# A row of norm weights spread by two matmuls with ones, in place of a load into all partitions

## The chip, the cores and the metric

One core of one Trainium2 chip runs the whole kernel. The metric is the device time of one execution in microseconds (us), of which the median over runs is given. The profile is one execution's, taken by the hardware profiler.

## The reference

One layer of a hybrid decoder trunk. 16 learned meta tokens are put ahead of 1,024 tokens of 1,024 channels; every token is normalised, and all groups (difference attention, a short gated convolution, a Mamba-2 scan) read the result through one projection:

```python
def rmsnorm(x, w):
    xf = x.astype(jnp.float32)
    y = xf * lax.rsqrt(jnp.mean(xf * xf, axis=-1, keepdims=True) + NORM_EPS)
    return (y * w.astype(jnp.float32)).astype(x.dtype)
...
    h = jnp.concatenate([meta, x], axis=1)
    for layer in range(DEPTH):
        u = rmsnorm(h, norm_w[layer])
        proj = jnp.einsum('bld,de->ble', u, w_in[layer])
...
        y = jnp.concatenate([y_attn, y_conv, y_ssm], axis=-1)
        h = h + jnp.einsum('ble,ed->bld', y, w_out[layer])
    return rmsnorm(h, final_norm_w)[:, N_META:]
```

`norm_w` is one row of 1,024 float32 values (4 KB), and every token's row is multiplied by it. Everything is float32 at the interface.

## The kernel before, in words

The program has three parts: a token stage that is run once (the table `AHEAD`), a loop of four iterations over heads (`BODY` three times and `LAST`), and the output projection. Each engine walks the same table in order and takes from it the steps that are its own; an engine never changes that order, and semaphores do the rest.

The token stage turns the tokens into the transposed, normalised matrix that all projections read, as a high part `u_hi` and a low part `u_lo`. It works on nine token tiles, numbered 0 to 8: tile 0 is the 16 meta tokens, tiles 1 to 8 have 128 tokens each, one per partition. For tile `a` the steps are:

- `x_load` (SP, L756): the DMA of the tile into `x_buf[a]`, 512 KB (64 KB for tile 0). The buffers are parts of `acum_b`, `work`, `lm_buf` and `ys`, and have these names in the profile.
- `x_square` (ScalarE, L1000): squares, summed along the row.
- `x_mean` (VectorE, L1202): 1/1024 of the sum, plus epsilon.
- `x_power` (GpSimd, L895): to the power -1/2.
- `x_scale` (VectorE, L1208): the tile times this factor, times `norm_row`, the norm's weights, which must be there in every partition. Called the first scaling for tile 0, the second for tile 1.
- `x_turn` (TensorE, L1584): eight transposes into PSUM.
- `x_high` (ScalarE, L1007) and `x_low` (VectorE, L1212): `u_hi` and `u_lo`.

`ahead()` writes the table: first the loads, in the order in which SP issues them, then rounds `r`, in each of which `PIPE` puts the steps of neighbouring tiles side by side (`x_square` three tiles ahead, `x_mean` and `x_power` two, `x_scale` and `x_turn` one). `BETWEEN` adds the first weight tiles and the first projections (`project`, L1599, into the PSUM banks `pb[0]` and `pb[1]`).

```python
PIPE = (("x_high", 0), ("x_square", 3), ("x_scale", 1), ("x_mean", 2), ("x_low", 0), ("x_power", 2), ("x_turn", 1))
```

`norm_row` is a part of `conv_u`, filled by the step `norm_load` (SP, L758), a DMA that writes the 4 KB row into all 128 partitions. Only the first scaling waits for it (`norm_in`). The constants (identity, `ones` and others) are written by GpSimd at the start, each adding one to `consts`; TensorE waits for all eight before its first instruction.

Of the kernel before, what the change touches and what calls it, by code (L numbers as in the profile page):

```python
# [15 lines left out]
P = 128  # L16
D = 1024
# [18 lines left out]
HALF = D // 2  # L36
# [119 lines left out]


def ahead():
    out = [("x_load", 0, 1), ("x_load", 1, 1), ("norm_load", 0, 1), ("x_load", 2, 1), ("x_load", 3, 1), ("load", 0, 1),
           ("x_load", 4, 1), ("load", 1, 1), ("w_dt_load", 0, 1)]  # L160
    out += [("x_load", a, 1) for a in range(5, CH)] + [("params_load", 0, 1)]
    for r in range(-3, CH):
        for name, lead in PIPE:
            if 0 <= r + lead < CH:
                out.append((name, r + lead, 1))
        out += [(name, arg, 1) for name, arg, at in BETWEEN if at == r]
    return out + [(name, arg, 1) for name, arg in BEHIND]

# [180 lines left out]
BODY = schedule(False)  # L349
LAST = schedule(True)  # L350
AHEAD = ahead()
DVE_OWN = 76
class Chain:
# [30 lines left out]
def build(nc, x, meta_tokens, norm_w, w_in, w_out, attn_lambda, attn_norm_w, sconv_w, ssm_conv_w,  # L384
# [6 lines left out]
    with ExitStack() as ctx:  # L391
        def sb(name, shape, dt=F32):
            return ctx.enter_context(nc.sbuf_tensor(name, shape, dt))

        def sem(name):
            return ctx.enter_context(nc.semaphore(name))
# [51 lines left out]
        th_piece = sb("th_piece", [P, 2, T // 2])  # L448
# [40 lines left out]
        s_tmp = [ys[:, n, HALF * m:HALF * (m + 1)] for n in range(2) for m in range(2)]  # L489

        norm_row = gate[:, 0:D]

        x_buf = [acum_b[:, :, :, :].rearrange("p b r n -> p (b r n)"), prob[0], prob[1], xs_flat[:, 0:LP], xs_flat[:, LP:2 * LP],
                 raw[:, 3:3 + LP], lm_buf[:, 3:3 + LP], ys[:, 0, :], ys[:, 1, :]]
# [5 lines left out]
        ones = sb("ones", [P, P])  # L500
# [50 lines left out]
        pb = [ps[:, 0, :], ps[:, 1, :]]  # L551
# [12 lines left out]
        params_in = sem("params_in")  # L564
        x_in = [sem(f"x_in{b}") for b in range(CH)]
        norm_in = sem("norm_in")
        w_dt_in = sem("w_dt_in")
        consts = sem("consts")
        x_sq = sem("x_sq")
# [144 lines left out]
        def _(eng):  # L714
# [24 lines left out]
            def iteration(i, steps):  # L739
                for step, a, d in steps:  # L740
# [12 lines left out]
                    elif step == "x_load":  # L753
                        n = META if a == 0 else P
                        src = meta_tokens if a == 0 else x_rows[(a - 1) * P:a * P, :]
                        eng.dma_start(x_buf[a][0:n, 0:D], src).then_inc(x_in[a], 16)  # L756
                    elif step == "norm_load":
                        eng.dma_start(norm_row, norm_w[0, :].partition_broadcast(P)).then_inc(norm_in, 16)  # L758
                    elif step == "w_dt_load":
                        eng.dma_start(w_dt, w_in_t[:, :, C_DT:C_DT + SH]).then_inc(w_dt_in, 16)  # L760
                    elif step == "params_load":
# [55 lines left out]
                    elif step == "t_store":  # L817
                        j = it * T_PAIRS + a
                        eng.wait_ge(t_ok, 4 * j + 4)
                        for m, name in enumerate(SUMS):  # L820
                            row = (m * KS + j) * P
                            eng.dma_start(t_dram[row:row + P, :], t_buf[name]).then_inc(t_st, 16)

            iteration(-1, AHEAD)
            for i in range(0, HEADS - 1):
                iteration(i, BODY)
            iteration(HEADS - 1, LAST)


# [123 lines left out]
        def _(eng):  # L953
# [24 lines left out]
            def iteration(i, steps):  # L978
                for step, a, d in steps:
                    it = i + d  # L980
                    if step == "split":
# [8 lines left out]
                        if a in SHARED:  # L990
                            eng.copy(w_hi[:, b, 0:KD // 2, :], w_raw[:, b, 0:KD // 2, :]).then_inc(w_half_ok, 1)
                            eng.copy(w_hi[:, b, KD // 2:KD, :], w_raw[:, b, KD // 2:KD, :]).then_inc(w_hi_ok, 1)
                        else:
                            eng.copy(w_hi[:, b, :, :], w_raw[:, b, :, :]).then_inc(w_hi_ok, 1)  # L994
                    elif step == "x_square":
                        n = META if a == 0 else P
                        eng.wait_ge(x_in[a], 16)
# [68 lines left out]
                    elif step == "gate_taps":  # L1066
                        n = a - TXS0
# [9 lines left out]
                    elif step == "exp":  # L1077
                        s, m = a
# [23 lines left out]
                    elif step == "z":  # L1102
                        p = PZ + a - 1
                        eng.wait_ge(piece_done, it * PPI + p + 2)
                        eng.activation(th_piece[:, p % 2, 0:GW], pb[p % 2][:, 0:GW], ACT.Tanh, scale=0.5).then_inc(zth_ok, 1)
                    elif step == "norm":
                        n = it * QB + a
# [5 lines left out]
                    elif step == "ssm_out":  # L1113
                        n = it * QB + a
# [6 lines left out]
                    elif step == "out_slot":  # L1121
# [4 lines left out]
                        high_w(a)  # L1126

            iteration(-1, AHEAD)
            for i in range(0, HEADS - 1):
                iteration(i, BODY)  # L1130
            iteration(HEADS - 1, LAST)

            def square(t, second):
# [39 lines left out]
        def _(eng):  # L1173
# [18 lines left out]
            def iteration(i, steps):  # L1192
                for step, a, d in steps:
                    it = i + d
                    if step == "parameters":

                        eng.wait_ge(par_tr, 1)
                        own(eng, eng.tensor_copy(par[:, :], o_ps[:, 0:R_END]))
                    elif step == "x_mean":
                        n = META if a == 0 else P  # L1200
                        eng.wait_ge(x_sq, a + 1)
                        eng.tensor_scalar(ms[0:n, a:a + 1], ss[0:n, a:a + 1], 1.0 / D, EPS, ALU.mult, ALU.add).then_inc(x_ms, 1)  # L1202
                    elif step == "x_scale":
                        n = META if a == 0 else P
                        eng.wait_ge(x_rs, a + 1)
                        if a == 0:
                            eng.wait_ge(norm_in, 16)
                        eng.scalar_tensor_tensor(x_buf[a][0:n, 0:D], x_buf[a][0:n, 0:D], rs[0:n, a:a + 1], norm_row[0:n, :], ALU.mult, ALU.mult).then_inc(x_n, 1)  # L1208
                    elif step == "x_low":
                        ca, cb = token_cols(a)  # L1210
# [127 lines left out]
                    elif step == "taps":  # L1338
                        t, j = a
                        n = t - TXS0  # L1340
# [15 lines left out]
                    elif step == "gate_taps":  # L1356
                        n = a - TXS0
# [6 lines left out]
                    elif step == "scores":  # L1364
                        s, m = a
                        nk = P * (s + 1) + META
                        n = it * 2 * QB + 2 * s + m
# [68 lines left out]
                    elif step == "chunk":  # L1436

                        n = META if a == 0 else P
# [19 lines left out]
                    elif step == "z":  # L1458

                        p = PZ + a - 1  # L1460
# [6 lines left out]
                    elif step == "scan":  # L1467
# [7 lines left out]
                        if a > 0:  # L1475
# [7 lines left out]
                            p = PZ + a - 1  # L1483
# [5 lines left out]
                    elif step == "norm":  # L1489

                        eng.wait_ge(z_sq, it * QB + a)
                        eng.tensor_scalar(z_ms[:, a % 2:a % 2 + 1], z_ss[:, a % 2:a % 2 + 1], 0.25 / GW, EPS, ALU.mult, ALU.add).then_inc(z_ms_ok, 1)

            iteration(-1, AHEAD)
            for i in range(0, HEADS - 1):
                own.begin(i)
                iteration(i, BODY)
                own.end()
            own.begin(HEADS - 1)
            iteration(HEADS - 1, LAST)  # L1500
            own.end()

# [49 lines left out]
            for n in range(5, 7 * KS):  # L1552
                p, j = n // KS, n % KS
# [28 lines left out]
        def _(eng):  # L1582
# [62 lines left out]
            def iteration(i, steps):  # L1645
                for step, a, d in steps:
                    it = i + d
                    if step == "project":
                        p, h = a
# [19 lines left out]
                                      range(h * KD // 2, (h + 1) * KD // 2))  # L1669
                        if h == 1:  # L1670
                            ins.then_inc(piece_done, 1)
                    elif step == "x_turn":
                        n = META if a == 0 else P
                        eng.wait_ge(x_n, a + 1)
# [52 lines left out]
                    elif step == "scores":  # L1727
                        s, m = a
                        n = it * 2 * QB + 2 * s + m
# [42 lines left out]
                    elif step == "chunk":  # L1772
                        n = META if a == 0 else P
# [13 lines left out]
                    elif step == "z":  # L1787

                        p = PZ + a - 1
# [12 lines left out]
                    elif step == "scan":  # L1802
                        n = META if a == 0 else P
# [23 lines left out]
                    elif step == "ssm_out":  # L1827
# [3 lines left out]
                        turn(yt_ps[:, P:2 * P], y_n[:, a % 2, P:2 * P]).then_inc(y_tr, 1)  # L1831

            iteration(-1, AHEAD)
            for i in range(0, HEADS - 1):
                iteration(i, BODY)
            iteration(HEADS - 1, LAST)


# [30 lines left out]
```

## Time and profile before

| | us |
|---|---|
| median of 3 runs | 1050.74 (1050.49 to 1052.12) |
| profiled execution | 1049.79 |
| its span | 1048.1 |
| TensorE busy in the span | 1013.8 (97%) |
| VectorE busy | 665.6 (64%) |
| ScalarE busy | 401.8 (38%) |
| GpSimd busy | 253.8 (24%) |

The span runs from the first to the last recorded instruction; the profiled execution's own time is 1.69 us longer. Times within the profile count from the start of the span. PE is TensorE's matmul, PEld its weight load, DVE VectorE, ACT ScalarE, POOL GpSimd, and SPq the queue of SyncE that issues DMAs. L12 is line 12 of the kernel. A matmul's duration is modelled to its end and overlaps the next one's; the distance between two starts tells the rate.

### The profile page before, as it was taken

The page shows a single profiled execution, that of the slowest core. Times are in us where ns is not written, and L with a number is a line of the kernel's source. Part 1 is how long each engine was busy: PE and PEld are TensorE (multiplying, and loading weights), DVE is VectorE, ACT ScalarE, POOL GpSimd, SP SyncE. Part 2 cuts the span into 40 slices and gives each one's busy share as a digit, 9 for nine tenths or more (in the row PEclk, how much of TensorE's full clock was granted, in tenths as well). Part 3 has the DMA queues.
Part 4 walks back from the last instruction along what each step waited for, and adds up shares of the span by engine and source line. Part 5 has one row for each costly group of instructions (what it writes and reads, how often), then busy time and mean ns, then how long its engine had stood idle before and what let it go on. Part 6 is the DMA issues. An engine that isn't in the chain of part 4 may idle for free.

```text
span 1048.1 us, 16326 instructions
## 1 busy us (share of the span) xinstructions
PE 1013.8 (97%) x6177; PEld 924.9 (88%) x6177; DVE 665.6 (64%) x1327; ACT 401.8 (38%) x892; POOL 253.8 (24%) x222
## 2 busy tenths in 40 slices
PE   4999999999999999999999999999999999999996
PEld 3889989898999898989999989899999898888885
DVE  7555767557257674672576756724767646798866
ACT  6333442233444332334343222343442233544554
POOL 3012331333223312332224133222241330000002
PEclk9999999999999999999999999999999999999999
DMA  8012322221142222211422322114223203994313
GB/s 268 1 44 81 101 81 71 71 61 44 47 133 101 71 81 71 61 41 41 141 84 76 93 71 61 42 41 141 76 70 101 71 20 105 359 389 140 100 51 161
DMA packets 105945, 101.22 MB, mean 97 GB/s; under 512 B 6022, under 2 KB 79852, under 8 KB 105868
## 3 DMA queue, kind: packets, MB, share of 16 engines
q1 hardware_dynamic: 105868, 100.18, 30.0%
q8 instruction: 50, 0.82, 0.3%
q14 instruction: 27, 0.22, 0.1%
HBM read 79.11 MB, written 21.05 MB: 96 GB/s over the span
## 4 chain that ended last, share of the span: by engine, by line
PE 84%; DVE 7%; issue 3%; DMA 2%; ACT 2%; POOL 1%; SPq 0%; POOLq 0%; DVEq 0%; ACTq 0%
PE ps L1599 43%; PE ps L1608 13%; PE ps L1800 9%; PE ps L1584 5%; PE ps L1765 3%; DVE lm_buf L1433 2%; PE ps L1814 2%; DMA acum_b<-acum_scratch 2%; PE ps L1743 2%; PE ps L1744 2%; PE ps L1816 1%; PE ps L1820 1%; PE ps L1691 1%; PE ps L1766 1%; DMA conv_u<-in_norm_w 1%
## 5 line engine op out<-in xcount | busy, mean ns | idle before, releaser
L1599 PE MATMUL ps<-u_hi,w_hi 128*128 128x348 f32 (+3 forms) x1024 | 364.4, 356 | 6.7 <-ACT conv_b_s L1053 2.5
L1599 PE MATMUL ps<-u_lo,w_hi 128*128 128x348 f32 (+3 forms) x1024 | 348.3, 340 | 0.0
L1599 PE MATMUL ps<-u_hi,w_lo 128*128 128x348 f32 (+3 forms) x1024 | 347.7, 340 | 0.0
L1599 PEld LDWEIGHTS ps<-u_hi,w_hi 128*128 128x128 f32 x1024 | 194.0, 189 | 19.8 <-issue 5.5
L904 POOL TENSOR_TENSOR w_lo<-w_raw,w_hi 128x1024 fp32r<-128x1024 f32 (+1 forms) x56 | 123.1, 2197 | 346.2 <-ACT w_hi L994 274.4
L1599 PEld LDWEIGHTS ps<-u_hi,w_lo 128*128 128x128 f32 x1024 | 193.3, 189 | 10.9
L1599 PEld LDWEIGHTS ps<-u_lo,w_hi 128*128 128x128 f32 x1024 | 193.7, 189 | 10.3
L895 POOL TENSOR_TENSOR small<-small,m_half 128x1 f32<-128x1 f32 (+2 forms) x57 | 41.5, 729 | 338.9 <-DVE small L1545 144.8
L1372 DVE TENSOR_REDUCE small<-ps 128x1 f32<-128x144 f32 (+7 forms) x64 | 49.5, 774 | 95.8 <-PE ps L1747 95.3
L1800 PE MATMUL ps<-w_hi,u_hi 128*128 128x256 f32 x256 | 73.1, 286 | 0.0
L1800 PE MATMUL ps<-w_lo,u_hi 128*128 128x256 f32 x256 | 72.0, 281 | 0.0
L1800 PE MATMUL ps<-w_hi,u_lo 128*128 128x256 f32 x256 | 72.0, 281 | 0.0
L1086 ACT ACTIVATE work<-ps,small 128x144 f32<-128x144 f32 (+7 forms) x64 | 48.0, 751 | 53.7 <-DVE small L1372 53.7
L1584 PE MATMUL ps<-ident,work 128*128 128x128 f32 (+2 forms) x369 | 56.6, 288 | 6.1 <-DVE work L1208 6.1
L1608 PE MATMUL ps<-q_hl 128*128 128x512 f32 x264 | 62.1, 389 | 0.0
L1433 DVE TENSOR_SCALAR lm_buf<-acum_b,sg 128x128 f32<-128x128 f32 x128 | 44.5, 409 | 27.5 <-DMA acum_b<-acum_scratch 27.5
L1101 ACT ACTIVATE lm_buf<-lm_buf 128x512 f32<-128x512 f32 x32 | 20.2, 632 | 107.0 <-DVE lm_buf L1433 107.0
L1112 ACT ACTIVATE y_n<-y_n,small 128x256 f32<-128x256 f32 x32 | 16.3, 510 | 112.9 <-POOL small L895 112.9
L1608 PEld LDWEIGHTS ps<-q_hl 128*128 128x128 f32 x264 | 49.6, 188 | 10.3
L1584 PEld LDWEIGHTS ps<-ident,work 128*128 128x128 f32 (+2 forms) x369 | 44.4, 143 | 9.9 <-DVE work L1208 7.8
L1456 DVE TENSOR_TENSOR lm_buf<-lm_buf,cbm 128x512 f32<-128x512 f32 x32 | 22.6, 707 | 43.3 <-PE ps L1820 43.1
L994 ACT CAST w_hi<-w_raw 128x1024 fp32r<-128x1024 f32 x48 | 49.9, 1040 | 0.1
(302 smaller groups left out, 1768.7 us busy)
## 6 DMA issues: line engine op xcount, KB each, us to landing
w_raw<-in_w_in SPq DMA_DIRECT2D x56, 512.0 KB, 4.1
acum_b<-acum_scratch SPq DMA_DIRECT2D x32, 256.0 KB, 4.4
acum_b<-in_w_out SPq DMA_DIRECT2D x22, 256.0 KB, 4.3
work<-in_w_out SPq DMA_DIRECT2D x16, 256.0 KB, 4.0
t_scratch<-work SPq DMA_DIRECT2D x16, 256.0 KB, 2.3
t_scratch<-acum_b SPq DMA_DIRECT2D x16, 256.0 KB, 2.6
y_scratch<-ys SPq DMA_DIRECT2D x8, 512.0 KB, 4.0
work<-in_x SPq DMA_DIRECT2D x4, 1024.0 KB, 8.4
```

The lines of the kernel that those rows point to most:

```text
L895: return eng.tensor_tensor(to[0:rows_, n:n + w], of[0:rows_, n:n + w], m_half[0:rows_, 0:w], ALU.pow)
L904: eng.tensor_tensor(w_lo[:, a % 2, ks, :], w_raw[:, a % 2, ks, :], w_hi[:, a % 2, ks, :].bitcast(F32), ALU.subtract).then_inc(w_lo_ok, 1)
L994: eng.copy(w_hi[:, b, :, :], w_raw[:, b, :, :]).then_inc(w_hi_ok, 1)
L1086: eng.activation(prob[m][:, 0:nk], s_ps[:, 0:nk], ACT.Exp, bias=mx[:, m:m + 1], accum_out=psum_e[:, s % 2, m:m + 1]).then_inc(exp_ok, 1)
L1372: eng.tensor_reduce(mx[:, m:m + 1], s_ps[:, 0:nk], AX.X, ALU.max, negate=True).then_inc(max_ok, 1)
L1433: ins = eng.tensor_scalar(lmat[:, a % 2, r, :], acum_b[:, a % 2, r, :], sg[:, 1, a, r:r + 1], 0.0, ALU.subtract, ALU.min)
L1456: eng.tensor_tensor(lmat[:, b, :, :], lmat[:, b, :, :], cbm[:, b, :].unsqueeze(1).to_broadcast([P, R, P]), ALU.mult).then_inc(g_ok, 1)
L1584: return eng.transpose(dst, src, ident[0:n, 0:n])
L1599: ins = eng.matmul(dst, w[:, k, 0:m], u[:, k, cols], start=(k == 0 and n == 0), stop=(k == KD - 1 and n == 2))
L1608: ins = eng.matmul(ps[:, BANKS[n // KS][t], :], y[:, at], w, start=(begins and m == 0), stop=(ends and m == 2), skip_group_check=True)
L1765: eng.matmul(o_ps[:, P:2 * P], a_t[:, n, :], v_blk[:, n, :], start=(n == 0), stop=False)
L1800: ins = eng.matmul(pb[p % 2][:, 0:GW], u[:, k, ca:cb], w[:, :, k, :], start=(k == 0 and n == 0), stop=(k == KD - 1 and n == 2))
```

## The change

`norm_load` now loads the row once, into partition 0 of `th_piece`, a buffer that is free at this time, and is the first load that SP issues. TensorE has a step of the same name: it waits for the row and makes two matmuls of float32 with `ones[0:1, :]` as weights (one row of 128 ones) and half of the row, 512 columns, as the moving operand, into `pb[0]` and `pb[1]`; so each half stands in all 128 partitions of PSUM. A new step `norm_copy` takes them to `norm_row`: ScalarE the first half, VectorE the second. The first scaling waits for both copies (`norm_ok`) instead of for the DMA.

```diff
 def ahead():
-    out = [("x_load", 0, 1), ("x_load", 1, 1), ("norm_load", 0, 1), ("x_load", 2, 1), ("x_load", 3, 1), ("load", 0, 1),
+    out = [("norm_load", 0, 1), ("x_load", 0, 1), ("x_load", 1, 1), ("x_load", 2, 1), ("x_load", 3, 1), ("load", 0, 1),
...
             if 0 <= r + lead < CH:
                 out.append((name, r + lead, 1))
+            if (name, r + lead) == ("x_square", 0):
+                out.append(("norm_copy", 0, 1))
...
+        norm_one = th_piece[0:1, :, :].rearrange("p a n -> p (a n)")
...
                     elif step == "norm_load":
-                        eng.dma_start(norm_row, norm_w[0, :].partition_broadcast(P)).then_inc(norm_in, 16)
+                        eng.dma_start(norm_one, norm_w).then_inc(norm_in, 16)
...
+                    elif step == "norm_copy":
+                        eng.wait_ge(norm_pe, 1)
+                        eng.copy(norm_row[:, 0:HALF], pb[0][:, :]).then_inc(norm_ok, 1)
...
+                    elif step == "norm_copy":
+                        eng.wait_ge(norm_pe, 2)
+                        eng.tensor_copy(norm_row[:, HALF:D], pb[1][:, :]).then_inc(norm_ok, 1)
...
                         if a == 0:
-                            eng.wait_ge(norm_in, 16)
+                            eng.wait_ge(norm_ok, 2)
...
+                    elif step == "norm_load":
+                        eng.wait_ge(norm_in, 16)
+                        for m in range(2):
+                            eng.matmul(pb[m][:, :], ones[0:1, :], norm_one[:, m * HALF:(m + 1) * HALF], start=True, stop=True).then_inc(norm_pe, 1)
```

Of the table's order the places that matter are shown as it stands on each engine, with the semaphores that an instruction waits for. VectorE at the start of the token stage, before:

```order
L1181 CAST ident_b<-ident 128x128 [waits consts]
L1202 TENSOR_SCALAR small<-small 16x1 [waits x_sq,dve_own]
L1208 SCALAR_TENSOR_TENSOR acum_b<-acum_b,small,conv_u 16x1024 [waits norm_in,x_rs]
L1202 TENSOR_SCALAR small<-small 128x1 [waits x_sq]
L1208 SCALAR_TENSOR_TENSOR work<-work,small,conv_u 128x1024 [waits x_rs]
```

And in the changed kernel (the mean is now L1213, the scaling L1219):

```order
L1189 CAST ident_b<-ident 128x128 [waits consts]
L1209 COPY conv_u<-ps 128x512 [waits norm_pe,dve_own]
L1213 TENSOR_SCALAR small<-small 16x1 [waits x_sq]
L1219 SCALAR_TENSOR_TENSOR acum_b<-acum_b,small,conv_u 16x1024 [waits norm_ok,x_rs]
L1213 TENSOR_SCALAR small<-small 128x1 [waits x_sq]
L1219 SCALAR_TENSOR_TENSOR work<-work,small,conv_u 128x1024 [waits x_rs]
```

The copy of the second half stands ahead of the mean of tile 0, because the table has `norm_copy` right behind the square of tile 0. Everything behind it is in the order of before.

ScalarE in the changed kernel, from its table load (the square is now L1008):

```order
L1008 ACT_TABLE_LOAD
L1008 ACTIVATE th_tile,small<-acum_b 16x1024 [waits x_in0]
L1002 COPY conv_u<-ps 128x512 [waits norm_pe]
L1008 ACTIVATE conv_y,small<-work 128x1024 [waits x_in1]
L1008 ACTIVATE th_tile,small<-work 128x1024 [waits x_sq,x_in2]
```

The copy of the first half is the only new row; it stands between the squares of tiles 0 and 1. TensorE has the two matmuls ahead of the transposes of tile 0 (L1595), in the changed kernel:

```order
L1686 MATMUL ps<-th_piece,ones 128x512 [waits norm_in,consts]
L1686 MATMUL ps<-th_piece,ones 128x512
L1595 MATMUL ps<-ident,acum_b 128x16 [waits x_n]
L1595 MATMUL ps<-ident,acum_b 128x16 x7
L1595 MATMUL ps<-ident,work 128x128 [waits x_n]
```

Nothing else moved on TensorE.

## Rows read from the trace of the kernel before

**Rows 1.** The page, part 1: busy time of TensorE, share of the span.

```profile
PE 1013.8 (97%) x6177; PEld 924.9 (88%) x6177; DVE 665.6 (64%) x1327; ACT 401.8 (38%) x892; POOL 253.8 (24%) x222
```

**Rows 2.** The chain that ended last, 0 to 26 us: start us, us, what.

```profile
1.72 5.41 DMA conv_u<-in_norm_w
...
7.23 1.27 DVE acum_b L1208
...
9.24 1.29 DVE work L1208
...
10.58 1.98 PE ps L1584 x8
...
13.49 1.13 ACT th_tile L1000 x2
...
23.67 1.97 PE ps L1584 x8
```

**Rows 3.** Windows: us; PE, PEld, DVE, ACT, POOL busy; granted clock, DMA share, GB/s.

```profile
6.00:8.00 2.00, 0.00 (x0) 0.00 (x0) 0.77 (x1) 0.56 (x2) 0.00 (x0) 1.00 0.99 385
8.00:10.00 2.00, 1.00 (x8) 0.92 (x8) 1.33 (x3) 1.46 (x4) 0.55 (x1) 1.00 1.06 362
...
46.00:55.00 9.00, 9.00 (x56) 7.91 (x54) 5.58 (x15) 1.54 (x4) 0.00 (x0) 1.00 0.01 2
```

**Rows 4.** Timeline of ScalarE: start us, us, what [idle before <-releaser].

```profile
5.41 1.06 ACT L1000 ACTIVATE conv_y<-work 128x1024 f32<-128x1024 f32 x1 [1.33 <-DMA work<-in_x]
...
8.52 1.06 ACT L1000 ACTIVATE th_tile<-work 128x1024 f32<-128x1024 f32 x1 [1.96 <-DMA work<-in_x]
```

**Rows 5.** Timeline of SyncE's queue: the issues of DMAs.

```profile
0.80 0.40 SPq L756 DMA_DIRECT2D acum_b<-in_meta_tokens  x1
1.26 0.41 SPq L756 DMA_DIRECT2D work<-in_x  x1
...
3.81 1.44 SPq L756 DMA_DIRECT2D work<-in_x  x1
...
16.25 0.26 SPq L766 DMA_DIRECT2D conv_g<-in_attn_norm_w  x1
```

**Rows 6.** DMA issues at 0.80 and 3.81: size, us from issue to landing.

```profile
acum_b<-in_meta_tokens SPq DMA_DIRECT2D x1, 64.0 KB, 2.1
...
work<-in_x SPq DMA_DIRECT2D x1, 512.0 KB, 9.0
```

**Rows 7.** Timeline of VectorE: the means of tiles 0, 1 and 2.

```profile
4.19 0.14 DVE L1202 TENSOR_SCALAR small<-small 16x1 f32<-16x1 f32 x1 [0.48 <-ACT th_tile L1000]
...
8.44 0.14 DVE L1202 TENSOR_SCALAR small<-small 128x1 f32<-128x1 f32 x1
...
10.44 0.15 DVE L1202 TENSOR_SCALAR small<-small 128x1 f32<-128x1 f32 x1
```

**Rows 8.** Timeline of GpSimd: the last of the eight constants.

```profile
3.10 0.20 POOL L891 MEMSET v_meta<- 128x128 f32 x1
```

**Rows 9.** The chain at 62 us: one matmul of 144 columns, float32, with `ones`.

```profile
62.49 0.24 PE ps L1709 x2
```

**Rows 10.** Timelines of weight loads and of TensorE, 28 to 32 us.

```profile
28.05 0.33 PEld L1599 LDWEIGHTS ps<-u_lo,w_hi 128*128 128x128 f32 x1
28.34 0.33 PEld L1599 LDWEIGHTS ps<-u_hi,w_lo 128*128 128x128 f32 x1
...
30.50 0.19 PEld L1599 LDWEIGHTS ps<-u_lo,w_hi 128*128 128x128 f32 x1
30.66 0.19 PEld L1599 LDWEIGHTS ps<-u_hi,w_lo 128*128 128x128 f32 x1
...
31.94 1.03 PE L1584 MATMUL ps<-ident,ys 128*128 128x128 f32 x8
```

**Rows 11.** Groups by shape, 0 to 140 us: copies of 512 columns from PSUM.

```profile
L1363 DVE COPY conv_b_s<-ps 128x512 f32<-128x512 f32 x1 | 0.7, 690 | 1.6 <-PE ps L1584 1.6
...
L1075 ACT COPY conv_b_s<-ps 128x512 f32<-128x512 f32 x1 | 0.6, 587 | 2.6 <-DVE conv_b_s L1363 2.6
```

More of the change, by code:

```diff
@@ L566, in build @@
         norm_in = sem("norm_in")
+        norm_pe = sem("norm_pe")
+        norm_ok = sem("norm_ok")
         w_dt_in = sem("w_dt_in")
```

## The prediction, written before the changed kernel ran

> **What bounds the kernel now.** The page comes first: TensorE is busy 97% of the span [rows 1], so time can be won or lost only where TensorE does not run back to back, and the change touches the first 10 us, where it does not. The chain of waits of that stretch [rows 2] is to be read from the top: the last thing waited for before any arithmetic is the load of the norm's weights into all partitions, 1.72 to 7.13 us; then the first scaling on VectorE (7.23), by way of GpSimd's power the second scaling (9.24), eight transposes of token tile 1 (10.58), and from 13.49 a chain of ScalarE and VectorE steps with no DMA in it, up to the transposes at 23.67 and the first projection behind them, at 25.3. From there TensorE has no gap for 30 us; the windows show it busy in all of 46 to 55 [rows 3]. The first scaling is thus the gate of the start: what it moves moves the first projection, as long as the steps behind it keep their order, which they do.
>
> Two things in that chain must be seen. First, DMA leaves it at 7.13. The square of token tile 2 starts at 8.52, and before it ScalarE idles 1.96 us for the data [rows 4]; but that square feeds a mean that starts at 10.44 [rows 7], behind the second scaling. Token tile 4 is issued at 3.81 and takes 9.0 us [rows 5, 6], so it is there at 12.8, and its square starts at 13.49, after the high part of tile 1. Second, VectorE is in order: the mean of tile 1 (8.44) stands behind the first scaling, though its square ended by 6.5 [rows 4, 7].
>
> **The change, part by part.**
>
> *The load.* Removed is 512 KB out of a stream that moves 362 to 385 GB/s [rows 3]; at that rate it is 1.4 us, and 1.4 us lie between the landing of this load (7.13) and of tile 2 (8.5). Every later landing comes some 1.4 us earlier, less about 0.3 us because the row's issue now stands first on SP's queue (a one-row load keeps that queue 0.26 us, one of 128 rows 0.41 [rows 5]). This is worth nothing: what is waited for after 7.13 in the chain is no DMA, and the cover is ScalarE's and VectorE's own work. Were a landing in the chain, the gain would be at most 1.1 us.
>
> *The row.* 4 KB in one partition, issued at 0.80, where the meta tokens' load was. Those 64 KB took 2.1 us [rows 6], the nearest row; the far bound is the 4.1 us of token tile 1 (issued at 1.26, square at 5.41 [rows 4, 5]). I take 2.1: there at 2.9. The matmuls also wait for the eight constants, the last written by 3.30 [rows 8]. So they start at 3.4, and the row has 0.4 us in hand.
>
> *Two matmuls of 1x128 by 1x512, float32.* The trace has none of that size. The nearest is the one with the same ones matrix, 144 columns in float32: 0.24 us for one (recorded as two) late in the program [rows 9]. By columns 512 cost 0.85 us. But that is at full clock. The windows print a granted clock of 1.00 at 6 to 10 us too [rows 3], and the spacing of the instructions says otherwise: the weight loads of matmuls of 348 columns start 0.29 us apart at 28 us and 0.16 apart at 30.5, and eight transposes take 1.97 us at 23.67 and 1.03 at 31.94 [rows 2, 10]. 348 columns in 0.29 us is 1.2 GHz, and in 0.15 it is 2.4. The engine had run transposes on and off since 8.65 and without a pause since 23.67 when the rate changed. So the low level holds at 3.4 us, and a matmul costs 1.7. Bounds: 0.85 and 1.7 each; I take 1.7, since all of TensorE's work before 28.9 ran at it. With the 0.2 us that a result takes to come out (eight transposes at 0.22 are 1.76 of the 1.97), the first is done at 5.3 and the second at 3.4 + 3.4 + 0.2 = 7.0.
>
> *The copies.* ScalarE's copy of the first half takes 0.59 us, VectorE's of the second 0.69 [rows 11]. ScalarE's runs from 5.3 to 5.9. Queued behind it is the square of tile 1, whose data comes at about 5.7 (issued 0.3 later); the square ends near 7.0, and its mean is not wanted before 9.7. Nothing lost. VectorE's is another matter: it stands **ahead of the mean of tile 0** (the order above), so that mean, the power behind it and the first scaling wait for the second matmul. In the kernel before that mean was done at 4.33 [rows 7], under cover of the load; that cover is gone. VectorE: copy 7.05 to 7.74; the mean starts at 7.7; from a mean's start to its scaling's start is 0.80 (8.44 to 9.24 [rows 2, 7]); first scaling at 8.5. From the first scaling to the second 2.0 us as before: 10.5 instead of 9.24.
>
> *Sum.* -0 (load), and +1.3 us on the second scaling, passed on whole: 8.5 - 7.23 = 1.27. The transposes, the projections and everything behind are the same instructions in the same order, with TensorE as their bound. The profiled execution took 1049.79 us for a span of 1048.1; with the change 1051.1. The median of the runs before lies 0.95 us above it, so the forecast for a median is 1050.74 + 1.3 = **1052.0 us**, 0.12% more. About 0.2% (2.1 us) is what a measurement of this kernel can tell from no change; the three runs before already lie 1.6 us apart. It counts as no change.
>
> **The rivals.**
>
> *A. The clock rises early.* The matmuls keep TensorE at work without a pause for 3.4 us before the transposes begin. If that lifts it to 2.4 GHz and it stays there, tile 1's transposes take 1.0 us less (+1.3 becomes +0.3), those at 23.67 another 1.0 less, and the 12 projections up to 28.9 take 0.13 less each, 1.6, with 0.3 on the transposes between: 0.3 - 1.0 - 1.6 - 0.3 = -2.6, so 1048.1. For it: when the rate did change, the projections had run 3.6 us (25.3 to 28.9), not much longer. Against it: transposes before them lifted nothing, and TensorE would stand idle from 7 to 9.8, when those of tile 0 start. If it helps tile 1's transposes alone, +0.3 is left: 1051.0. The Trainium skill, "TensorE: Matmul & The Clock Gate", Part 1, says that the throttled state is the default and that sustained matmul activity releases it; its Part 4 says that transposes do not count as such activity. The trace agrees so far as it goes: no transpose before 25.3 brought full rate, the projections did. By that rule the two new matmuls are the first activity that counts.
>
> *B. The matmuls run at full clock from the start.* Second one done at 3.4 + 1.7 + 0.2 = 5.3, copy to 6.0, first scaling at 6.8. The second waits for its own mean, behind the first scaling: 8.8, against 9.24. -0.4: 1050.3. Against it: every early row.
>
> *C. The row lands late (the case on the slower side).* It is the only thing that the matmuls wait for besides the constants, and only its landing can be later than 3.4. The row goes through the same queues as the loads behind it; if its last piece comes with the first big tile, 4.1 us after its issue as for tile 1, the matmuls start at 5.0 and all is 1.6 us later: +2.9, 1053.6. It decides from a landing at 4.2 us (+2.1). For it: no landing of a one-partition load is to be seen. Against it: the 64 KB landed in 2.1.
>
> *D. The clock rises later.* The projections start 1.3 us later; if the change of rate comes not 1.3 but some 12 projections later, these cost 0.13 each more: +1.3 + 1.6 = +2.9, again 1053.6. The reverse, a rise at the same time as before, takes half of the delay back (projections at half speed for 1.3 us less): +0.65, 1051.4.
>
> *E. The delay is absorbed.* If a step between 9.24 and 23.67 waits in truth for a load, the 1.1 us by which the loads come earlier take back most of the 1.3: 1050.9. The nearest is tile 4's square, whose data is there 0.7 us before it; that is against it, since the slack is on the wrong side.
>
> **How the numbers follow.** The forecast with its variants from +0.65 to +2.0: 0.62. B, E and the partial form of A, between -0.4 and +0.3: 0.13. A in full: 0.06. C: 0.08. D: 0.11. The range takes the forecast, B and the near halves of C and D, and leaves out A in full and the far halves: 1050.2 to 1053.6. Faster by over 0.2% is A in full, 0.06; slower by over 0.2% is C and D, 0.19; within is the rest, 0.75.
>
> **What would show it.** In the profile after: a matmul of 512 columns twice from 3.4 us, some 3.4 us together (B: 1.7); VectorE's copy at about 7.05 with the mean of tile 0 right behind it, instead of at 4.19; first scaling at 8.5, second at 10.5, the first projection at 26.6 instead of 25.3; the square of tile 2 no longer waiting until 8.5. C shows as TensorE idle beyond 3.5 for a DMA. A shows as the eight transposes of tile 1 in 1.0 us. D shows in the time at which 348 columns go from 0.29 to 0.16 apart. The prediction is wrong if the second scaling is not late, or if it is and the first projection is not.

## The result, and the profile after

| | us | ratio to before, 95% interval |
|---|---|---|
| before, 7 runs | 1051.03 (1050.06 to 1053.1) | |
| after, 7 runs | 1055.06 (1054.62 to 1055.46) | 1.0035 [1.0023, 1.0047] |

The kernel after is slower by 4.0 us; 1.3 had been predicted, and the range ended at 1053.6. The profiled execution took 1055.46 us for a span of 1053.7.

The page, part 1, of the kernel after; it answers to [rows 1]. The work is the same; of the 3.9 us more of TensorE, 3.75 are the two matmuls.

```profile
PE 1017.7 (97%) x6181; PEld 926.1 (88%) x6181; DVE 666.5 (63%) x1328; ACT 402.7 (38%) x893; POOL 254.2 (24%) x222
```

The chain of waits of the kernel after, from 3 us to the first projection, answers to [rows 2].

```profile
3.17 0.15 POOL v_meta L896
3.33 2.57 issue
5.90 3.76 PE ps L1686 x4
...
9.76 0.69 DVE conv_u L1209
10.45 0.06 DVE small L1213
...
10.65 0.55 POOL small L900
...
11.23 1.27 DVE acum_b L1219
...
13.23 1.30 DVE work L1219
...
14.57 1.98 PE ps L1595 x8
```

The DMA of 5.41 us is gone, and the new matmuls, the copy, the mean and the power stand in its place, as the prediction said. What it did not have is the second row: the last constant is written at 3.32, and then come 2.57 us of "issue", in which TensorE waits for nothing that the profile shows. It does not seem to wait for the row either. The windows of this kernel show when the row was moved (us; PE, PEld, DVE, ACT, POOL busy; granted clock, DMA share, GB/s): 20 GB/s for 0.2 us are 4 KB, the size of the row, and the next data comes after 2.0.

```profile
1.60:1.80 0.20, 0.00 (x0) 0.00 (x0) 0.20 (x1) 0.20 (x1) 0.09 (x1) 1.00 0.09 20
1.80:2.00 0.20, 0.00 (x0) 0.00 (x0) 0.20 (x1) 0.20 (x1) 0.08 (x1) 1.00 0.00 0
```

The trace's record of this one piece of 4,096 bytes runs from 1.72 to 2.02. A landing counts somewhat later than its last piece: in the kernel before the 16 pieces of the meta tokens end at 2.26 and the landing is at 2.9 [rows 6]. By that distance an estimate for the row is 2.7, before the last constant. The timelines of TensorE and VectorE (start, us, what, [idle before <-releaser]) give each step.

```profile
5.90 3.75 PE L1686 MATMUL ps<-th_piece,ones 1*128 1x512 f32 x4 [5.90 <-issue]
...
14.57 3.98 PE L1595 MATMUL ps<-ident,work 128*128 128x128 f32 x16 [0.99 <-DVE work L1219]
20.10 1.10 PE L1595 MATMUL ps<-ident,work 128*128 128x128 f32 x8 [1.54 <-DVE work L1219]
...
29.28 0.64 PE L1610 MATMUL ps<-u_hi,w_hi 128*128 128x348 f32 x1
```

```profile
9.76 0.69 DVE L1209 COPY conv_u<-ps 128x512 f32<-128x512 f32 x1 [6.04 <-PE ps L1686]
10.37 0.13 DVE L1213 TENSOR_SCALAR small<-small 16x1 f32<-16x1 f32 x1
11.23 1.27 DVE L1219 SCALAR_TENSOR_TENSOR acum_b<-acum_b,small,conv_u 16x1024 f32<-16x1024 f32 x1 [0.73 <-POOL small L900]
...
13.23 1.28 DVE L1219 SCALAR_TENSOR_TENSOR work<-work,small,conv_u 128x1024 f32<-128x1024 f32 x1 [0.67 <-POOL small L900]
```

| us from the span's start | before | predicted | after |
|---|---|---|---|
| matmuls start | - | 3.4 | 5.90 |
| VectorE's copy | - | 7.05 | 9.76 |
| mean of tile 0 | 4.19 | 7.7 | 10.37 |
| first scaling | 7.23 | 8.5 | 11.23 |
| second scaling | 9.24 | 10.5 | 13.23 |
| first projection | 25.29 | 26.6 | 29.28 |

From the copy down every line is about 2.7 us behind the prediction, and 2.5 of that are there when the matmuls start. The 4.0 us of the last line are the 4.0 of the medians.

The two profiled executions lie 5.7 us apart, 1.7 more than the medians, and TensorE's clock accounts for about as much. The windows at 60 to 72 us (us; PE, PEld, DVE, ACT, POOL busy; granted clock, DMA share, GB/s), of before and then of after, show a stretch at the lower of the two levels (1.00 is 2.4 GHz, 0.50 is 1.2 GHz) behind the wait for the sums of dt (L1708, L1723 after), in after only:

```profile
60.00:64.00 4.00, 2.00 (x14) 2.03 (x15) 2.84 (x9) 0.90 (x1) 2.36 (x1) 1.00 0.00 0
64.00:68.00 4.00, 4.00 (x30) 3.77 (x30) 2.23 (x5) 2.68 (x6) 1.05 (x1) 1.00 0.47 131
```

```profile
64.00:68.00 4.00, 2.42 (x12) 2.45 (x13) 2.54 (x7) 0.65 (x3) 2.35 (x1) 0.79 0.02 4
68.00:72.00 4.00, 4.00 (x24) 3.60 (x24) 1.40 (x3) 2.39 (x6) 0.32 (x1) 0.78 0.45 127
```

Short of 1.00 by 0.21 and 0.22 over 8 us makes 1.7 us of full-rate work lost. Whether the change brings this stretch or not is one of the questions below.

### The profile page after: what moved, and what is told of

Read it like the earlier page. It is cut to its first block, busy times and chain, and to the rows that moved or that the text cites. A ratio compares the mean times of both kernels' runs of the same rounds, so it can differ in the third digit from the quotient of the medians.

```text
span 1053.7 us, 16336 instructions
## 1 busy us (share of the span) xinstructions
PE 1017.7 (97%) x6181; PEld 926.1 (88%) x6181; DVE 666.5 (63%) x1328; ACT 402.7 (38%) x893; POOL 254.2 (24%) x222
## 4 chain that ended last, share of the span: by engine, by line
PE 84%; DVE 7%; issue 3%; DMA 2%; ACT 2%; POOL 1%; SPq 0%; POOLq 0%; DVEq 0%; ACTq 0%
PE ps L1610 43%; PE ps L1619 13%; PE ps L1815 9%; PE ps L1595 5%; PE ps L1780 3%; DVE lm_buf L1444 2%; PE ps L1829 2%; DMA acum_b<-acum_scratch 2%; PE ps L1758 2%; PE ps L1759 2%; PE ps L1831 1%; PE ps L1835 1%; PE ps L1706 1%; PE ps L1781 1%; PE ps L1762 0%
## 5 line engine op out<-in xcount | busy, mean ns | idle before, releaser
L1595 PE MATMUL ps<-ident,work 128*128 128x128 f32 (+2 forms) x369 | 55.7, 285 | 7.1 <-DVE work L1219 7.0
L1595 PEld LDWEIGHTS ps<-ident,work 128*128 128x128 f32 (+2 forms) x369 | 43.7, 141 | 10.7 <-DVE work L1219 8.6
```

What stands on the lines that cost most here:

```text
L1595: return eng.transpose(dst, src, ident[0:n, 0:n])
```

## The experiments

**Theory 1** for the 2.57 us: TensorE's own queue. Ahead of its first wait stand 32 `sem_inc` instructions that hand out the semaphores of buffers which are free at the start (`w_lo_ok`, the list `primed`, `raw_free`, `primed_dma`). They had been hidden behind the wait for tile 0, until 8.65 us. **Rival**: something of the matmuls themselves, such as the first use of the engine, or the row's arrival after all. Each kernel ran beside the kernel before, whose median was 1050.19 us (1049.44 to 1052.23) where no other is given.

### The matmuls ahead of the increments

```diff
             eng.sem_inc(w_lo_ok, 2)
+            eng.wait_ge(consts, 8)
+            eng.wait_ge(norm_in, 16)
+            for m in range(2):
+                eng.matmul(pb[m][:, :], ones[0:1, :], norm_one[:, m * HALF:(m + 1) * HALF], start=True, stop=True).then_inc(norm_pe, 1)
             for guard in primed:
                 eng.sem_inc(guard, 1)
             eng.sem_inc(raw_free, 1)
             for guard in primed_dma:
                 eng.sem_inc(guard, 16)
-            eng.wait_ge(consts, 8)
```

(and the step `norm_load` of TensorE is taken out of the table's loop)

> The changed kernel with the two matmuls ahead of TensorE's 31 priming semaphore increments (only the one that SyncE waits for stays ahead). Theory 1 (the 2.5 us between the last constant and the first matmul, 3.3 to 5.9, are TensorE working through its own increments): matmuls start at 3.4, second scaling at 10.7 instead of 13.23, first projection at 26.8 instead of 29.3, median 2.5 below the changed kernel's, about 1052.5. Theory 2 (the first matmul needs those 2.5 us itself, fetching instructions or starting up) and theory 3 (the row lands only at 5.8): start stays at 5.9, the time stays at 1055.

1052.07 us (1051.35 to 1053.96, 9 runs), ratio 1.0018 [1.0009, 1.0028]. TensorE's timeline, then VectorE's:

```profile
3.36 3.77 PE L1602 MATMUL ps<-th_piece,ones 1*128 1x512 f32 x4 [3.36 <-POOL v_meta L896]
```

```profile
7.25 0.69 DVE L1209 COPY conv_u<-ps 128x512 f32<-128x512 f32 x1 [3.53 <-PE ps L1602]
7.85 0.13 DVE L1213 TENSOR_SCALAR small<-small 16x1 f32<-16x1 f32 x1
8.71 1.27 DVE L1219 SCALAR_TENSOR_TENSOR acum_b<-acum_b,small,conv_u 16x1024 f32<-16x1024 f32 x1 [0.73 <-POOL small L900]
```

The matmuls now wait for the last constant and nothing else, and 2.5 us are back. The row was in place by then, and the matmuls take 3.77 us as against 3.75, so the rival is out: neither the row nor the engine's first use holds them. The first projection starts at 26.75, where the prediction had 26.6, and +1.9 us of the median (0.9 to 2.9 by the interval) hold the predicted +1.3. The prediction was in effect a prediction of this kernel.

### The price of an increment by itself

The kernel before, with 31 more increments of a semaphore that nobody waits for.

```diff
             for guard in primed_dma:
                 eng.sem_inc(guard, 16)
+            for _ in range(31):
+                eng.sem_inc(spare, 1)
             eng.wait_ge(consts, 8)
```

> The kernel before with 31 more semaphore increments (of a semaphore that nobody waits for) on TensorE behind its 32 priming ones, ahead of its first wait. If each costs what the changed kernel's start says, (5.87 - 0.75) / 32 = 0.16 us, TensorE is free at 10.8 instead of 5.9, the transposes of tile 0 start there instead of at 8.65, those of tile 1 at about 11.9 instead of 10.58, and the time rises by 1.3 us to 1051.5. If increments are nearly free (20 ns) nothing changes and another cause must be found for the 2.5 us.

1051.14 us (1050.31 to 1052.59, 10 runs) beside before at 1050.41: 1.0007 [0.9998, 1.0016]. TensorE's timeline:

```profile
10.64 1.00 PE L1585 MATMUL ps<-ident,acum_b 16*128 16x16 f32 x8 [10.64 <-DVE work L1209]
11.57 3.91 PE L1585 MATMUL ps<-ident,work 128*128 128x128 f32 x16
17.09 1.97 PE L1585 MATMUL ps<-ident,work 128*128 128x128 f32 x8 [1.61 <-DVE work L1209]
```

Tile 0's transposes start at 10.64 instead of 8.65, although their input was ready as before. The kernel with the filler matmuls below has them right behind the 32 increments, at 5.74; 31 more end at 10.64, which makes 4.90 / 31 = 0.16 us for one, and 32 of them 5.1 us. (Reckoned from the 5.90 of the kernel after, whose matmuls have one wait more ahead of them, as the transposes have here, it is 0.15.) So TensorE was free in the kernel before from about 5.8 us, with 2.9 us of cover left (8.65 less 5.74). The delay of 1.99 at tile 0 becomes 0.99 at tile 1 (11.57, before 10.58), and that is passed on: the third group starts at 17.09 instead of 16.10, and the first projection at 26.27 instead of 25.29. Expected were +1.3 us; the trace shows +0.98, and the median's +0.7 agrees with that, but can't be told from nothing. As the row also shows, the releaser in the brackets (VectorE's scaling) is inferred: it names a producer, where the engine was held by its own queue.

### The mean ahead of the copy

```diff
-            if (name, r + lead) == ("x_square", 0):
+            if (name, r + lead) == ("x_mean", 0):
                 out.append(("norm_copy", 0, 1))
```

> The changed kernel with the copies behind the mean of tile 0 in the table. If VectorE's order costs what the prediction said, the mean of tile 0 is at 4.4, the first scaling follows the copy at 10.5 instead of 11.23, and the time is 0.75 us below the changed kernel's (1054.3). If only the matmuls' end counts, no change.

1054.0 us (1053.69 to 1054.07, 5 runs), 1.0037 [1.0024, 1.0049]. VectorE's timeline:

```profile
4.48 0.14 DVE L1213 TENSOR_SCALAR small<-small 16x1 f32<-16x1 f32 x1 [0.76 <-ACT th_tile L1008]
9.69 0.69 DVE L1209 COPY conv_u<-ps 128x512 f32<-128x512 f32 x1 [5.06 <-PE ps L1686]
10.49 1.27 DVE L1219 SCALAR_TENSOR_TENSOR acum_b<-acum_b,small,conv_u 16x1024 f32<-16x1024 f32 x1
```

Mean and power are back under cover, and the scaling follows the copy at once: 10.49 instead of 11.23, first projection 28.54 instead of 29.28. That is 0.74 us, the price of the order alone. The median, 1.1 lower than that of after in another set of runs, doesn't contradict it and can't resolve it.

### Both, and the mean of tile 1 ahead of the first scaling; the same in the kernel before

The first has the two edits above and this one; the second is the kernel before with this one alone.

```diff
+    for name in ("x_mean", "x_power"):
+        out.remove((name, 1, 1))
+        out.insert(out.index(("x_scale", 0, 1)), (name, 1, 1))
     return out + [(name, arg, 1) for name, arg in BEHIND]
```

> Matmuls ahead of the increments, copies behind the mean of tile 0, and the mean and power of tile 1 ahead of the first scaling. Theory 1: matmuls 3.4 to 7.15, first scaling at 7.9, second at 9.15, so the time of the kernel before (1051). Theories 2 and 3: first scaling at 10.5, second at 11.8, 2.5 us above the kernel before.

> The kernel before (load into all partitions) with only the mean and power of tile 1 ahead of the first scaling. If the gate is the first scaling and what stands behind it on VectorE, the second scaling starts at 8.5 instead of 9.24 and the time falls by 0.75 us to about 1050.3, unless a data landing or the clock takes it back.

The first took 1050.56 us (1049.46 to 1051.35, 11 runs), 1.0002 [0.9993, 1.0011]; the second 1049.66 (1048.26 to 1050.6, 11 runs), 0.9996 [0.9987, 1.0005]. VectorE's timeline of the first, then of the second:

```profile
7.17 0.69 DVE L1212 COPY conv_u<-ps 128x512 f32<-128x512 f32 x1 [2.51 <-PE ps L1605]
7.78 0.14 DVE L1216 TENSOR_SCALAR small<-small 128x1 f32<-128x1 f32 x1
7.97 1.29 DVE L1222 SCALAR_TENSOR_TENSOR acum_b<-acum_b,small,conv_u 16x1024 f32<-16x1024 f32 x1
9.19 1.27 DVE L1222 SCALAR_TENSOR_TENSOR work<-work,small,conv_u 128x1024 f32<-128x1024 f32 x1
```

```profile
6.89 0.15 DVE L1205 TENSOR_SCALAR small<-small 128x1 f32<-128x1 f32 x1 [2.59 <-ACT conv_y L1003]
7.13 1.27 DVE L1211 SCALAR_TENSOR_TENSOR acum_b<-acum_b,small,conv_u 16x1024 f32<-16x1024 f32 x1
8.33 1.27 DVE L1211 SCALAR_TENSOR_TENSOR work<-work,small,conv_u 128x1024 f32<-128x1024 f32 x1
```

With tile 1's power ready, the second scaling follows the first after 1.2 us instead of 2.0. With all three edits the matmul route brings the first projection to 25.21, level with before (25.29); the same last edit on the load's route brings it to 24.39. So the best that was made of the route by matmuls is 0.8 us behind the load with the same order: the copy ends at 7.86, while the load had landed by 7.13. Neither kernel's time can be told from before.

### TensorE's clock: warm-up and the gap at the sums of dt

The kernel before with the mean of tile 1 first (the one just above, 1049.66 us) gets five filler matmuls (128 columns, `ones` by `ones`, into a bank that is overwritten afterwards) ahead of the transposes of tiles 0, 3, 4 and 5; the next kernel has these and eight more ahead of the wait for the sums of dt; the last is the kernel before with these eight alone. Before ran beside them at 1050.41 us (1049.64 to 1052.17). No result is changed by the fillers.

```diff
+            def fill(bank, n):
+                for _ in range(n):
+                    eng.matmul(ps[:, bank, 0:P], ones[:, :], ones[:, :], start=True, stop=True)
...
                     elif step == "x_turn":
                         n = META if a == 0 else P
+                        if a in (0, 3, 4, 5):
+                            fill(1, 5)
                         eng.wait_ge(x_n, a + 1)
...
                     elif step == "dt_cum":
+                        fill(3, 8)
                         eng.wait_ge(adt_ok, 1)
```

> The previous experiment without matmuls for the row (load kept, mean of tile 1 ahead of the first scaling) plus five filler matmuls of 128 columns on ones before the transposes of tiles 0, 3, 4 and 5. If the clock rises once TensorE is kept busy from 5.9 us on, transposes of tile 5 take 1.0 instead of 2.0 us and the first 12 projections 0.16 apart instead of 0.29: first projection at 23.4 instead of 24.4 and all in all 2.5 us less than without fillers, about 1047.2. If the clock stays down, the fillers cost up to 0.6 us per gap (2.1 us at half rate in gaps of 1.5 to 1.9): 1050 to 1051.

> The same with eight fillers more in TensorE's wait of 2.3 us ahead of the sums of dt (60 us). If the half-rate stretch of 3.4 us that the records show behind this wait (66.4 to 69.8 in the changed kernel) comes from the idling, it disappears: no second fall of the clock, up to 1.7 us less in those executions that had it, 0.9 to 1.7 less in the median, about 1046. If it comes from something else, no change.

> The kernel before with only the eight fillers in the wait ahead of the sums of dt. If the fall of the clock behind this wait is what spreads the runs of the kernel before (1049.4 to 1053.1), the median falls by about 0.8 to 1.2 us and no fall is recorded before 1000 us; if not, the same as before.

| | us | ratio |
|---|---|---|
| mean of tile 1 first, fillers at the start | 1047.58 (1045.56 to 1048.3, 7 runs) | 0.9972 [0.9961, 0.9982] |
| the same, and fillers at the gap | 1045.84 (1045.68 to 1046.18, 5 runs) | 0.9959 [0.9946, 0.9971] |
| before, fillers at the gap alone | 1049.15 (1047.82 to 1052.03, 11 runs) | 0.9989 [0.998, 0.9998] |

TensorE's timeline of the first of these (fillers are L1600), which has the start of the fillers behind the 32 increments and then the transposes of tiles 1 and 2 together, of tile 3 and of tile 4:

```profile
5.74 2.47 PE L1600 MATMUL ps<-ones 128*128 128x128 f32 x10 [5.74 <-issue]
...
9.75 4.03 PE L1587 MATMUL ps<-ident,work 128*128 128x128 f32 x16 [0.17 <-DVE work L1211]
...
15.27 1.09 PE L1587 MATMUL ps<-ident,work 128*128 128x128 f32 x8
...
18.96 1.09 PE L1587 MATMUL ps<-ident,work 128*128 128x128 f32 x8 [1.48 <-DVE work L1211]
```

In the trace's records of the granted clock the full rate begins at 14.5 us and holds through the token stage, and eight transposes take 1.09 us from then on instead of 1.97. The first projection starts at 23.70, against 24.39 without the fillers. Of the 2.8 us by which this kernel is below before, 0.5 came in the median with the order alone (1049.66 beside 1050.19), so that about 2.3 are the fillers'; 2.5 had been expected. Rival A had priced full rate through this stretch at 3.9 us (1.0, 1.0, 1.6 and 0.3). Windows of this kernel and of the next at the gap:

```profile
56.00:60.00 4.00, 1.71 (x9) 1.51 (x8) 2.61 (x9) 1.40 (x2) 2.35 (x1) 0.86 0.01 2
60.00:64.00 4.00, 4.00 (x24) 3.78 (x23) 1.11 (x4) 1.98 (x6) 0.00 (x0) 0.71 0.47 131
```

```profile
56.00:60.00 4.00, 3.50 (x28) 3.33 (x27) 2.83 (x9) 1.41 (x2) 2.36 (x1) 1.00 0.01 2
```

With TensorE kept at work through the wait, the clock does not fall, and 1.7 us more are gained, as much as the stretch costs by its windows. Two of the seven runs without the gap's fillers, 1045.56 and 1045.62, lie where this kernel lies, and the other five at 1047.4 or above; they would be the ones without the stretch, but they have no trace. This kernel is the fastest of all, 4.6 us below before and 9 below the change. The gap's fillers alone gain 1.3 us in the median. Their profiled execution, the slowest of its eleven, has no fall at the gap but one at 205.8 to 209.2 us:

```profile
204.00:208.00 4.00, 3.02 (x14) 3.05 (x14) 0.85 (x4) 2.25 (x7) 0.61 (x1) 0.73 0.35 92
208.00:212.00 4.00, 4.00 (x24) 3.90 (x23) 1.42 (x5) 0.03 (x1) 0.56 (x1) 0.84 0.01 2
```

TensorE had idled 2.04 us before 204.98, for a ScalarE copy (L1053). The expectation, no fall before 1000 us, did not hold, but the idling went with it: in the other profiles TensorE waits for this copy 0.6 to 1.0 us, and the clock does not fall there.

Over all thirteen profiles of this document, between 40 us and the last twenty of the kernel, TensorE pauses for 2 us or more twelve times: this once, and 2.28 to 2.43 us ahead of the sums of dt in each of the eleven profiles without fillers there. Behind ten of the twelve comes a stretch of 3.4 us at the lower level, and nowhere else in that time. The two without are the first profile of before and that of the 31 more increments; what decides between the two outcomes is open.

### Before and after, profiled again

Does the stretch behind the sums of dt belong to the change? Both kernels unchanged, before twice and after once.

> The kernel before, unchanged, profiled once more. Theory 1 (the half-rate stretch behind TensorE's wait for the dt sums, at 62 to 70 us, comes in some executions of every kernel, and the first profile of before was one without it): a granted clock of 1.2 GHz for about 3.4 us behind 62 us, and a time near 1051.5; the first projection at 25.3 as in the first profile. Theory 2 (the stretch belongs to the changed kernel, whose wait is 2.42 us and not 2.30): no fall of the clock behind 62 us, time near 1049.8.

> The kernel before a third time. Theory 1: in one of three profiles or more of before there is a half-rate stretch of about 3.4 us behind 62 us, and those that have it take about 1.7 us more than those that do not. Theory 2: in none.

> The changed kernel, unchanged, profiled once more. Theory 1 (the stretch comes in some executions of every kernel): it may or may not be there; without it the time is near 1053.5, with it near 1055.5. Theory 2 (the stretch belongs to the changed kernel): half rate from about 66.4 to 69.8 us again. By both the norm's matmuls start at 5.9, the first scaling at 11.23 and the first projection at 29.3.

Before took 1049.96 and 1051.16 us, after 1054.42 (one execution each; spans 1048.2, 1049.4 and 1052.7). Windows of the two of before, then of after:

```profile
60.00:64.00 4.00, 2.90 (x12) 2.93 (x13) 2.07 (x7) 0.41 (x2) 2.35 (x1) 0.67 0.07 15
64.00:68.00 4.00, 4.00 (x27) 3.78 (x27) 1.71 (x4) 2.27 (x5) 0.63 (x1) 0.91 0.39 116
```

```profile
60.00:64.00 4.00, 2.50 (x13) 2.53 (x14) 2.47 (x7) 0.76 (x3) 2.37 (x1) 0.84 0.01 2
64.00:68.00 4.00, 4.00 (x24) 3.41 (x23) 1.82 (x4) 2.31 (x5) 0.75 (x1) 0.73 0.45 129
```

```profile
64.00:68.00 4.00, 2.99 (x11) 3.02 (x12) 1.99 (x6) 0.33 (x2) 2.20 (x1) 0.63 0.11 27
68.00:72.00 4.00, 4.00 (x28) 3.78 (x28) 1.78 (x4) 2.35 (x5) 0.71 (x1) 0.94 0.35 104
```

The stretch is there in both, so it is not the change's: the first profile of before was the one of three without it, and both of after have it. The kernel after repeats its start to 0.01 us (matmuls at 5.90, first projection at 29.29), and with the stretch on both sides the difference is 1054.42 less the mean of 1049.96 and 1051.16: 3.9 us, against 4.0 by the medians and 4.0 at the first projection. All three executions were faster than expected for one with the stretch (1051.5 for before, 1055.5 for after). The price of the stretch read off these executions is rougher than by its windows: before with it is 0.2 and 1.4 us longer than without, after the sums of dt had started 0.9 and 0.5 us earlier (61.10 and 61.50, against 62.00); that makes 1.1 and 1.9. These earlier starts come with the rise of the clock, which is in the records 4.1 us after the first projection's start in the first profile of before, 1.7 and 3.5 us in the others, and 2.9 and 1.6 in the two of after: each us earlier gives half of one back. The half us that is left between executions was not followed.

## Why the prediction was wrong

**The step that failed** is the sentence "So they start at 3.4, and the row has 0.4 us in hand." It took the constants and the row for all that the matmuls wait for, as rival C did too, and as the account of the kernel before does where it says that TensorE waits for the constants before its first instruction: that wait is the first one, but 32 instructions stand ahead of it. TensorE's queue had these 32 increments to go through, 0.16 us each, and was not free before about 5.8; the matmuls started at 5.90. The error is 2.5 us, and all the rest of the miss is about 0.2. The instructions stand in the code, but they do not count as busy in any view, and no wait before showed them, since the engine's first work came 2.9 us after their end. The kernel with the matmuls ahead of them shows it, and the one with 31 more gives the price. No rival of the prediction had this step. Whether the change can be told from none hung on it: +1.3 is below the 2.1 us that the prediction took for that, +4.0 above.

**The load, costed at nothing**: held. The squares no longer wait for DMA after the first (that of tile 2 starts right behind that of tile 1, at 9.5), and the first projection gains nothing from it.

**The row at 2.9 by the nearest row, 64 KB**: not refuted. Its bytes were moved by 2.02, and it was there by 3.36, when the kernel with the matmuls first started them. Rival C (the row late) is out.

**Two matmuls at 1.2 GHz, 3.6 us with the way out**: 3.75 and 3.77 in the two kernels. Rival B (full clock) is out, and with it the reading of the printed 1.00 in this stretch. Before the first clock record of a trace the windows print 1.00, whatever the rate; durations must be used.

**The copy ahead of the mean**: held. From the copy's start to the first scaling 1.45 were predicted and 1.47 came; the mean ahead gives back 0.74.

**Passed on whole to the first projection**: held to 0.1 us, in the kernel after (+4.0 and +4.0) and in the others. Rival E (absorbed) is out.

**The clock**: rival A in full did not come. TensorE worked 3.75 us on the norm's matmuls, and tile 1's transposes, at 14.57, still took 1.98 for eight. The records of after do have full rate from 18.6 to 22.0, and tile 3's transposes go in 1.10; but that is behind 4.0 us of transposes, and the projections come 7 us later at the low level again. It was worth nothing: tile 4's transposes start at 23.78 with this early rise and, in the second profile of after, without it, and the first projection at 29.28 and 29.29. Such a rise of 3.4 us stands in four of the five profiles that have the norm's matmuls, and in one of the six that have the load and no fillers at the start. Whether the two matmuls make it more likely is open. They are not needed for it: the one of six is the profile with the gap's fillers alone, which has nothing but transposes by then. TensorE's timeline of that kernel:

```profile
10.53 3.98 PE L1584 MATMUL ps<-ident,work 128*128 128x128 f32 x16 [0.92 <-DVE work L1208]
16.06 1.09 PE L1584 MATMUL ps<-ident,work 128*128 128x128 f32 x8 [1.54 <-DVE work L1208]
```

The prediction weighed the Trainium skill, "TensorE: Matmul & The Clock Gate", Part 4, by which TensorE's transpose mode does not count as activity for the clock in the way that matmuls do. If the transposes here are of that mode, which no view says, these rows speak against it: the full rate came at 14.7 us behind transposes alone. The measurement decides, and the prediction's "transposes before them lifted nothing" was true of the first profile of before and not of all. Part 1 of the Trainium skill's same page says that sustained matmul activity releases the throttle. The trace with the fillers agrees: full rate from 14.5 us until 58.9, where the five profiles of the load without early rise or fillers have it first at 27.2 to 30.7.

Rival D (the rise later) did not come: the rise is 2.9 and 1.6 us behind the first projection in the two profiles of after, and 4.1, 1.7 and 3.5 in the three of before. Half of the 2.4 us of spread, 1.2, is what executions of before alone differ by, so that D's +1.6 could hardly be told from it.

## What to carry to other kernels

When work is put first on an engine that used to start late, read everything that the engine's program has ahead of it: register, branch and semaphore instructions are in no busy time, and here 32 of them held TensorE for 5.1 us behind a wait that hid them. Ask of every hidden wait what else it hides; "issue" in the chain of waits is where such an instruction shows once it is uncovered. And a 512 KB load whose landing is 7.1 us into the kernel is not beaten by 4 KB and two float32 matmuls at the low clock, 3.75 us with a copy behind them; the larger prize lay in the clock, by a few filler matmuls in TensorE's pauses: with them in five places 4.0 us, besides 0.5 for an order on VectorE.

## What was not expected of the hardware

- A semaphore increment that stands by itself on TensorE's queue takes 0.15 to 0.16 us (31 of them 4.90 us by one reckoning, 4.74 by the other).
- Eight transposes take 1.97 us at the low level and 1.09 at the high one, and a float32 matmul of one row by 512 columns 1.88 us at the low one.
- Transposes alone (5.0 us of them from 8.6 to 14.5) were followed by the full clock at 14.7 us in one of six profiles that are alike up to there or differ in the start by 2 us at most; the other five had it only behind projections.
- Ten of twelve pauses of 2.0 to 2.4 us in TensorE's otherwise full work were followed by 3.4 us at half rate, worth 1.7 us. Pauses of up to 1.2 us were not. Five matmuls ahead of each of four groups of transposes, eight in the pause at the sums of dt and a mean moved forward on VectorE took 4.6 us off the kernel.
